# Opening of a streaming-encoder step on one core: constant matmuls ahead of x, transpositions first, low parts from the accumulator bank, first unit tile by tile

## What is computed

```python
x = x + 0.5 * swiglu(rms_norm(x, norm_g[layer, 0]), ffn_w_gate[layer, 0], ffn_w_up[layer, 0], ffn_w_down[layer, 0])
def swiglu(h, w_gate, w_up, w_down):
    return (jax.nn.silu(h @ w_gate) * (h @ w_up)) @ w_down
def rms_norm(x, g):
    return x * lax.rsqrt(jnp.mean(x * x, axis=-1, keepdims=True) + EPS) * g
```

## Time and profile before

| | |
|---|---|
| median of 3 runs | 2062.52 us |
| the profiled execution | 2060.64 us |
| its span in the profile | 2058.8 us |
| TensorE matmul busy | 2039.2 us (99%), 13866 matmuls |
| VectorE busy | 1476.8 us (72%) |
| ScalarE busy | 809.5 us (39%) |
| GpSimd busy | 547.3 us (27%) |
| HBM | 159.01 MB read, 4.00 MB written |

### The profile page before, as it was taken

How to read it: one execution, slowest core, us unless ns; L and a number is a source line. 1 busy time by engine, 2 the same in 40 slices (tenths; PEclk the granted TensorE clock), 3 DMA queues, 4 the chain that set the end, 5 groups by cost and what they waited for, 6 DMA issues and landing times. The chain is left out here.

```text
span 2058.8 us, 34279 instructions
## 1 busy us (share of the span) xinstructions
PE 2039.2 (99%) x13866; PEld 2004.4 (97%) x13866; DVE 1476.8 (72%) x2292; ACT 809.5 (39%) x1342; POOL 547.3 (27%) x382
## 2 busy tenths in 40 slices
PE   8999999999999999999999999999999999999998
PEld 6999999999889999999999999999999999999998
DVE  6896684974665579758487789576677888576685
ACT  5343342442433434334244344243335534333343
POOL 4243232402000025323240134232320045232230
PEclk9999999999999999999999999999999999999999
DMA  5233232333221223323223323323243123323222
GB/s 155 64 86 92 73 98 67 83 100 91 57 60 44 72 62 86 84 77 102 68 81 84 88 57 82 103 62 88 77 118 85 43 66 83 88 77 93 72 57 82
DMA packets 312004, 165.22 MB, mean 80 GB/s; under 512 B 15339, under 2 KB 309431, under 8 KB 311848
## 3 DMA queue, kind: packets, MB, share of 16 engines
q1 hardware_dynamic: 309152, 158.36, 27.8%
q0 software_dynamic: 2576, 4.64, 1.0%
q10 hardware_dynamic: 120, 0.04, 0.0%
HBM read 159.01 MB, written 4.00 MB: 79 GB/s over the span
## 5 line engine op out<-in xcount | busy, mean ns | idle before, releaser
L498 PE MATMUL psum<-xg_hi,in_hi 128*128 128x320 f32 x1952 | 611.3, 313 | 2.9 <-DVE in_lo L1212 2.4
L500 PE MATMUL psum<-xg_hi,in_lo 128*128 128x320 f32 x1952 | 604.5, 310 | 0.0
L499 PE MATMUL psum<-xg_lo,in_hi 128*128 128x320 f32 x1952 | 604.3, 310 | 0.0
L498 PE MATMUL psum<-f_hi,f_out_hi 128*128 128x320 f32 x1408 | 436.6, 310 | 2.1 <-DVE f_out_lo L1220 1.7
L500 PE MATMUL psum<-f_hi,f_out_lo 128*128 128x320 f32 x1408 | 435.1, 309 | 0.0
L499 PE MATMUL psum<-f_lo,f_out_hi 128*128 128x320 f32 x1408 | 435.1, 309 | 0.0
L498 PEld LDWEIGHTS psum<-xg_hi,in_hi 128*128 128x128 f32 x1952 | 367.4, 188 | 9.1 <-issue 3.3
L499 PEld LDWEIGHTS psum<-xg_lo,in_hi 128*128 128x128 f32 x1952 | 367.7, 188 | 0.6
L500 PEld LDWEIGHTS psum<-xg_hi,in_lo 128*128 128x128 f32 x1952 | 367.5, 188 | 0.0
L1662 POOL TENSOR_TENSOR sums<-in_raw 128x512 f32<-128x512 f32 x72 | 100.7, 1399 | 735.0 <-DVE in_lo L1224 474.5
L1224 DVE TENSOR_TENSOR in_lo<-in_raw,in_hi 128x1024 fp32r<-128x1024 f32 x144 | 233.0, 1618 | 55.8 <-ACT in_hi L893 55.8
(11 more groups left out here) (201 smaller groups left out, 2857.2 us busy)
## 6 DMA issues: line engine op xcount, KB each, us to landing
in_raw<-in_ffn_w_gate SPq DMA_DIRECT2D x88, 512.0 KB, 3.9
in_raw<-in_ffn_w_up SPq DMA_DIRECT2D x88, 512.0 KB, 5.2
out_raw<-in_ffn_w_down SPq DMA_DIRECT2D x96, 384.0 KB, 3.3
out_raw<-in_ffn_w_down SPq DMA_DIRECT2D x32, 256.0 KB, 3.0
in_raw<-in_mix_w_in SPq DMA_DIRECT2D x14, 512.0 KB, 4.5
out<-y_nat SPq DMA_DIRECT2D x5, 512.0 KB, 3.2
x_nat<-in_x_prompt SPq DMA_DIRECT2D x4, 512.0 KB, 5.8
in_raw<-in_mix_w_in SPq DMA_DIRECT2D x8, 256.0 KB, 4.6
```

The costliest lines, as they stand in the source:

```text
L498: pe.matmul(dst, w_hi, v_hi, start=first, stop=False)
L499: pe.matmul(dst, w_hi, v_lo, start=False, stop=False)
L500: return pe.matmul(dst, w_lo, v_hi, start=False, stop=last)
```

## The change

TensorE issues 16 constant matmuls (`mean_w` by `mean_w`, float32, 128 columns, bank 1) as soon as DVE has set `mean_w`. The vectors of weights arrive in two tensors: `norm_nat` is transposed ahead of x, `rest_nat` and the bias line's product behind the first four tiles of x. x's third tile is loaded in two halves, with chunk 0 behind the first. Unit 0 takes gate and up alternately for each k from k = 2 on; the second half's transpositions all move to unit 1; in ffn0, the units rotate over three pairs of banks. ACT makes `xg_hi` from the accumulator bank in place of `x`, and splits both tiles of chunk 0 behind tile 1 of x. DVE makes `xg_lo` from the accumulator bank, without the sum beside it; the sums of the squares are operations of their own (`start_sum`), eight of them behind the first `normalised`. POOL squares into eight buffers. Chunk 2's split goes ahead of `norm_factor` for half 1, and the split of the two tiles of `ffn_w_down` from behind unit 1's hidden tile to behind unit 2's on DVE.

```diff
+WARM = 16
-        sq_start = over("sq_start", [P, 2, HALF], A_HI + 17920)
+        sq_start = over("sq_start", [P, 8, HALF], A_HI + 768)
+        def in_bank(phase, u):
+            return 2 * (u % 3) if phase == "ffn0" else 2 * (u % 2)
...
-            for tile in (0, 1, 2):
-                load_x(tile)
+            for tile, hi in ((0, P), (1, P), (2, 64)):
+                load_x(tile, 0, hi, tile)
             load_ffn_in("ffn0", 0, 0, 0)
+            load_x(2, 64, P, 5)
...
             def turn_x(i):
-                wait(pe, x_ready, i - (3 if i < KT else 1))
+                wait(pe, xg_lo_done, i - (3 if i < KT else 1))
...
+            def first_unit():
+                for t, k in [(0, 0), (0, 1), (1, 0), (1, 1)] + [(t, k) for k in range(2, KT) for t in range(2)]:
+                    if t == 0:
+                        if k + 4 < KT:
+                            turn_x(k + 4)
+                        pe.wait_ge(xg_lo_done, k + 1)
+                    if k == 0:
+                        pe.wait_ge(in_split, t + 1)
+                    last = product(psum[:, t, 0:HALF], in_hi[:, 0, t, k], in_lo[:, 0, t, k],
+                                   xg_hi[:, k, cols(0)], xg_lo[:, k, cols(0)], k == 0, k == 7)
+                last.then_inc(in_mm, 1)
+            def between_first(q):
+                def between(t, k):
+                    if q == 1:
...
+                        if k % 2 == 0:
+                            turn_x(8 + 4 * t + k // 2)
+                        if (t, k) == (1, 2):
+                            pe.wait_ge(line_ready, 1)
+                            norm_mean(0, 0)
+                    if q == 2:
+                        if (t, k) == (0, 0):
+                            pe.wait_ge(xg_lo_done, 2 * KT)
+                    if q == 3 and (t, k) == (1, 0):
+                        pe.wait_ge(vec_ready, 2)
+                        norm_mean(0, 1)
...
+            pe.wait_ge(mean_ready, 1)
+            for _ in range(WARM):
+                pe.matmul(psum[:, 1, 0:P], mean_w[:], mean_w[:], start=True, stop=True)
             pe.wait_ge(pool_ready, 1)
...
             def start_tile(i):
                 act.wait_ge(x_turned, i + 1)
                 act.activation(x[:, d, cols(half)], psum[:, turn_bank(i), 0:HALF], ACT.Copy).then_inc(x_ready, 1)
-                act.wait_ge(x_ready, i + 1)
-                act.activation(xg_hi[:, d, cols(half)], x[:, d, cols(half)], ACT.Copy, scale=vec[:, d:d + 1]).then_inc(xg_hi_done, 1)
+                act.activation(xg_hi[:, d, cols(half)], psum[:, turn_bank(i), 0:HALF], ACT.Copy, scale=vec[:, d:d + 1]).then_inc(xg_hi_done, 1)
...
+            def start_low(i):
+                dve.wait_ge(xg_hi_done, i + 1)
+                dve.scalar_tensor_tensor(xg_lo[:, d, cols(half)], psum[:, turn_bank(i), 0:HALF], vec[:, d:d + 1],
+                                         xg_hi[:, d, cols(half)].bitcast(F32), ALU.mult, ALU.subtract).then_inc(xg_lo_done, 1)
+            def start_sum(i):
+                dve.wait_ge(sq_done, i + 1)
+                wait(dve, ss_done, i)
+                dve.tensor_tensor(ss[:, i // 8], ss[:, i // 8], sq_start[:, i % 8], ALU.add).then_inc(ss_done, 1)
...
+                        if (index, pair, q) == (0, 0, 2):
+                            in_lo_split((IN_CHUNK[phase] + b) % 2, SPLIT_CHUNK[phase] + q)
                         if pair == 0 and q in (0, 2) and (index, q) != (0, 0):
                             norm_factor(m, half)
...
-                        if pair == 0 and index == 0 and q == 1:
+                        if pair == 0 and index == 0 and q == 2:
                             out_lo_split(f_out_hi, f_out_lo, 0, 0, GROUPS[0])
                             out_lo_split(f_out_hi, f_out_lo, 1, 1, GROUPS[0])
...
+                            if (index, q) == (0, 0):
+                                for i in range(8, 16):
+                                    start_sum(i)
```

More of the change, by code:

```diff
@@ L566, in in_unit @@
+            def in_unit(c, slot, bank, u, half, between=None, read=1):
+                if u > 1:
                     wait(pe, in_split, 2 * c + 2)
-                wait(pe, in_read, u - 1)
+                wait(pe, in_read, u - read)
                 for t in range(2):
+                    if u == 1:
+                        pe.wait_ge(in_split, 2 * c + t + 1)
                     for k in range(8):
@@ L571, in in_unit @@
                             between(t, k)
-                        last = product(psum[:, 2 * j + t, 0:HALF], in_hi[:, slot, t, k], in_lo[:, slot, t, k],
+                        last = product(psum[:, bank + t, 0:HALF], in_hi[:, slot, t, k], in_lo[:, slot, t, k],
                                        xg_hi[:, k, cols(half)], xg_lo[:, k, cols(half)], k == 0, k == 7)
@@ L661, in _ @@
                 turn_x(i)
+            pe.wait_ge(vec_landed, 16 * 3)
+            pe.wait_ge(vec_ready, 1)
+            rest = V_ROWS - V_REST
+            pe.transpose(psum[:, 7, V_REST:V_ROWS], rest_nat[:, :], ident[0:rest, 0:rest]).then_inc(vec_turned, 1)
+            pe.wait_ge(const_landed, 32)
+            pe.matmul(psum[0:8, 6, 0:LINE], table[:, :], one_hot[:, :], start=True, stop=True).then_inc(line_mm, 1)
             pe.wait_ge(dve_ready, 1)
-            pe.wait_ge(line_ready, 1)
             ffn("ffn0", 0)
@@ L1073, in _ @@
+            act.wait_ge(in_landed[1], landed(1))
+            in_hi_tile(1, 0)
+            start_tile(8)
+            start_tile(9)
+            in_hi_tile(1, 1)
+            for i in (10, 11, 12):
                 start_tile(i)
             act.wait_ge(dve_ready, 1)
+            act.wait_ge(vec_ready, 2)
             rms(0, 0)
-            for i in range(12, 16):
+            for i in (13, 14, 15):
                 start_tile(i)
```

135 lines of the change are left out of this document (71 added, 64 removed).

## The result

| | before | after |
|---|---|---|
| median of 6 runs each | 2062.53 us (2060.51 to 2063.14) | 2069.82 us (2068.32 to 2072.15) |
| profiled execution / its span | 2060.64 / 2058.8 | 2069.92 / 2068.1 |

The ratio is 1.0037, with a 95% interval of 1.0024 to 1.0049: the change makes the kernel **slower, by 7.3 us**. The forecast was 2063.9, "no change that can be told" at 0.69. The time lies inside the range, the case that I held likeliest does not.

The account below looks back on a forecast made before the run. TensorE's matmuls are busy 99% of the span, but DVE's chain sets unit 5: 2.6 us won, then 28.9 for 24.9, so 67.6 for 66.2; 2062.5 + 1.4 = 2063.9 us, range 2061.0 to 2070.0.

Parts of the forecast that it names:

- no change that can be told: Whole kernel: a difference within the 0.2% (4.1 us) that a measurement can tell, given a chance of 0.69.
- the case that I held likeliest: Whole kernel: the forecast itself, +1.4 us to 2063.9, own range 2062.0 to 2064.9, chance 0.62.
- TensorE and DVE arrive together at unit 5: Unit 5 before the change: TensorE there at 66.1, DVE's split of chunk 3 done at 66.19.
- The two stalls in unit 1: TensorE in unit 1 waits for low parts: group 12 from 28.2 to about 29.2, group 15 for 2.4 us.
- The term for DVE's chain: From DVE's last low part to the end of chunk 3's split: 28.9 us in place of 24.9, ending at 67.6.
- DVE has its last low part at 38.7: End of DVE's opening: ready at 38.7, where before it was ready for unit 0's evacuation at 41.34, 2.6 us won.
- The clock falls before unit 0: Rival, opening: TensorE's clock falls between constant matmuls and first product; with 3 us lost +4.4, 2066.9; chance 0.20.
- The constants never bring the clock up: Rival, opening: constant matmuls end at 10.3, unit 0 starts near 15 and slowly; +6 to +8, 2069.5; chance 0.12.
- DVE is not the bound: Rival, units 4 and 5: unit 4's 4.8 us are kept and the kernel is faster, 2057.7; chance 0.06.
- Rule against row: Opening: the rule that transpositions don't count as TensorE's work gives 2066.9; the row at 2053 to 2055 gives 2063.9.

Follow-up runs that it names:

- run with chunk 3 first: The changed kernel with chunk 3's split moved from behind unit 3's hidden tile to behind unit 2's, on ACT and DVE: ratio 1.0020, median 2064.7 us.
- run with the clock held: The changed kernel with 16 more constant matmuls among x's transpositions and just ahead of the first product: ratio 1.0036, median 2068.0 us.
- run with 27 fillers: The changed kernel with 27 constant matmuls between units 4 and 5, ahead of the wait for chunk 3's split: ratio 1.0028, median 2068.7 us.
- runs with DVE's repairs: Changed kernel, chunk 3's split behind unit 2's hidden tile, four sums before low part 13, norm_factor behind low parts: 1.0002 without constant matmuls, 1.0000 with.
- five sums ahead: The changed kernel with five of the eight sums moved to DVE's idle stretch ahead of the first reciprocal: ratio 1.0038, median 2068.2 us.
- before with constants: The kernel before with the sixteen constant matmuls alone added at its start: ratio 0.9998, median 2060.4 us.

## Why the prediction was wrong

**What held.** TensorE and DVE arrive together at unit 5, and the shift of unit 5 is that of the end: chunk 3's split moved, TensorE stood 4.8 us in front of it (forecast about 6), and the run with chunk 3 first gave back half of the loss or more. That the wait had nearly its forecast length is luck: TensorE reached unit 5 7.6 us later than forecast (68.9 against 61.3) and DVE 6.1 us later (73.7 against 67.6). Unit 4, which should have started 4.8 us sooner than before, started 2.8 us later. The two stalls in unit 1 stood where they were put: before group 12 (1.5 us, forecast 1.0) and before group 15 (2.5, forecast 2.4). The term for DVE's chain was 28.9 and measured 29.6; a sum took 0.56, and one of the eight started 0.5 us late, where I had 0.52 each. What held that one up stays open: the row names only the sum ahead of it, and POOL's last square was done at 43.9. That the `ffn_w_down` split, the extra vector copy and POOL's buffers cost nothing is borne out in so far as no wait stands at them.

**The step that failed is "DVE has its last low part at 38.7".** It came to its end at 44.0, 5.3 us later, so that a gain of 2.6 became a loss of 2.7.

- 1.1 us: chunk 0's second tile landed at 11.7, where I had 10.8 by x's smaller piece in front of it, and unit 0 started at 14.2, not 13.1. (The 1.1 us that I halved for it were no distance between landings, but the difference of two durations in the earlier trace rows.)
- 3.5 us: the clock. I took 0.146 us for each matmul and 0.57 for each group; from 14.2 to 19.4 the matmuls stood 0.27 apart, and the groups, the products and the mean from 33.4 to 36.7 ran at half speed as well. The run with the clock held measures this at 3.5 us, and leaves 0.7 for everything else in the stretch; read stretch by stretch it is 3.8 and leaves 0.4.

**The second failed step is the one that is missing:** nothing was charged behind the wait before unit 5. The clock fell in that wait, and unit 5's first 4 us ran at 1.2 GHz: 2.0 us as half of the stretch, 1.9 by the run with 27 fillers. The errors are 5.3 + 0.7 + 2.0 = 8.0 us, against 7.9 between the forecast's +1.4 and the profile's +9.3.

**The rivals.** "The clock falls before unit 0" was the right mechanism, and its own arithmetic (half of the time between the fall and the return) was near for the first fall: 14.2 to 19.7 is 2.7 us, measured as 2.3. It fell short because it knew one fall, and there were four; of 0.20 it should have had most. "The constants never bring the clock up" is refuted: it rose at 6.0. "DVE is not the bound" is refuted by the wait before unit 5, and the runs with DVE's repairs come nearest to what it supposed: with 1.1 us of waits for splits and 1.8 for a hidden tile left there, the changed opening only reached the kernel before (1.0000 to 1.0002), not 2057.7.

**Rule against row.** I let the stretch from 2053 to 2055, 8 transpositions at a clock that was held, speak against the loss of the clock. That row came straight behind 2000 us of dense matmuls, and here the transpositions follow 6.2 us of constants. The 15 transpositions from 8.27 on still went at the high clock (12 in 2.33 us and 3 in 0.64, against 15 in 4.64), and the fall came at 12.9, 1.0 us after the last of them had ended, in the idle stretch. With matmuls between the same transpositions and in the idle stretch the clock held to 39.2. The Trainium skill, "TensorE: Matmul & The Clock Gate", Part 4: PE-mode transpose, has it that transpositions do not count as TensorE's work in the way that matmuls do; these runs agree with it in so far as matmuls among them kept the clock and transpositions with an idle stretch did not, but they do not part the two.

**Why little of the expected gain can arrive at all.** The change ends TensorE's first long wait, but unit 0 starts no sooner (14.2 us against 13.8), because it needs chunk 0 from HBM and its splits. From there DVE, not TensorE, has to go through sixteen low parts, sixteen sums, two reciprocals, four evacuations and the splits; whatever TensorE wins is stood through before unit 4 or 5. The change makes this order worse on DVE (eight sums stand inside the chain, while DVE idles 3.8 us in front of the reciprocal), and the low parts tie TensorE's transpositions to DVE (`xg_lo_done` in place of `x_ready`), which opens the stalls. That the tie itself is the cause of the falls at 33 and 43 is not shown: the low parts now read the bank, so the wait can't be taken away alone.

## What to carry to other kernels

Where two engines arrive at a unit together, look on the one that makes the operand for work that nobody needs yet and that stands ahead of it: here it was worth 2 to 3 us in the old kernel (two splits of weights) and 3.5 to 5 us in the new one (one split) to put them in front of an evacuation, while sixteen warm-up matmuls were worth under 1 us in either, which the runs can't tell from nothing. And when a forecast opens a stall of one or two us on TensorE in a stretch of transpositions, charge the matmuls behind it at half speed as a case of its own. Removing a stall can pay twice, for itself and for the clock.

## What the runs showed of the hardware

- The clock of a TensorE that had just been warmed up was easily lost: 16 constant matmuls of 6.2 us brought it up at 4 to 7 us in all ten kernels that had them, and in every one but that with matmuls among the transpositions it was low again between 10.9 and 13.9.
- A short stall can be followed by a low stretch or not, in the same code. All ten profiles of kernels with the changed opening have the stall of 1.5 us before group 12; the clock was low behind it in three (from 33.3, 33.4 and 34.1), not in the other seven. Before group 15 it was 2.5 to 3.2 us in seven of them, and in all seven the clock fell in it or within 2.1 us of its end; in the three with 1.0 us there it didn't.
- The wait of 2.44 us for chunk 2's split had no low stretch behind it in the profiled execution of the kernel before, and one from 58.3 to 61.7 in that of before with constants. With the wait taken away, the two groups of times of the kernel before became one. No execution of the upper group (2 to 3 us longer) was profiled, but each one's mean granted clock is on record: in the runs beside the experiments it is 0.999 or less in 30 of the 35 of the upper group, and 1.000 in 34 of the 43 of the lower. So the upper group is in the main the one in which the clock falls. Five of its executions show 1.000, and they stay unexplained; the record counts the time ahead of the first rise as high, so a later rise would not show. Where the clock falls in the others is not shown either: three profiles (27 fillers, five sums ahead, before with constants) have a low stretch of 3.4 us near 1580 to 1590 us, where all kernels run the same code and most had none.

```profile
1589.00:1594.00 5.00, 5.00 (x26) 4.61 (x24) 1.86 (x5) 1.25 (x3) 0.00 (x0) 0.66 0.00 0
```

- The place of the falls differs between executions of one code: with an unchanged opening, unit 0's evacuation came at 42.0, 42.7, 44.0 and 44.0 in four profiles. The changed kernel's six runs spread over 3.8 us, the kernel before's six beside them over 2.6, its 27 over 4.8: that more stalls make a kernel less steady is not shown.
- The recorded lows were of unequal length, from 3.4 us to 13.6 us (12.5 to 26.1, in a mixture of products and transpositions), so a single one can't be priced ahead. Half of its length, as far as TensorE had work in it, was near where it could be read: 2.7 against 2.3 us measured for the first, 1.7 against 1.5 for the second, 2.0 against 1.9 for the fourth.
